# First layer's second norm reordered on VectorE: latent chunks first, then a weight piece's low part, then the context's residual; halves of the output squares added on VectorE

## The reference

```python
def _rms_norm(x, g):
    xf = x.astype(jnp.float32)
    y = xf * lax.rsqrt(jnp.mean(xf * xf, axis=-1, keepdims=True) + EPS)
    return (y * g.astype(jnp.float32)).astype(x.dtype)

def _modulate(h, shift, scale):
    return h * (1 + scale) + shift
...
        y, yc = _even_mixer(...)                      # ends in "@ w_out" for latents (y) and context (yc)
        x = x + g1 * _rms_norm(y, norm_g[1])
        h2 = _modulate(_rms_norm(x, norm_g[2]), sh2, sc2)
        x = x + g2 * _rms_norm(ffn(h2), norm_g[3])    # ffn: (silu(h @ wg) * (h @ wu)) @ wd
        if need_ctx:
            ctx = ctx + cg1 * _rms_norm(yc, norm_g[1])
            hc2 = _modulate(_rms_norm(ctx, norm_g[2]), csh2, csc2)
            ctx = ctx + cg2 * _rms_norm(ffn(hc2), norm_g[3])
```

## Time and profile before

| | |
|---|---|
| median of 3 runs | 1662.55 us (1660.24 to 1663.87) |
| profiled execution, own time | 1663.6 us |
| its span | 1661.9 us |
| TensorE busy | 1615.5 us (97%) |
| VectorE busy | 1127.4 us (68%) |
| ScalarE busy | 928.7 us (56%) |
| granted TensorE clock, mean | 0.994 of full |

### The profile page before, as it was taken

One profiled execution on the slowest core, in us unless ns is written; L12 is line 12 of the kernel. 1 busy time (PEld: TensorE's weight loads), 2 busy tenths in 40 slices (PEclk: granted clock), 3 DMA queues, 4 the chain that ended last, 5 costly groups with the idle time before them and its releaser, 6 DMA issues.

```text
span 1661.9 us, 22634 instructions
## 1 busy us (share of the span) xinstructions
PE 1615.5 (97%) x8260; PEld 1298.2 (78%) x8260; DVE 1127.4 (68%) x1503; ACT 928.7 (56%) x1335; POOL 45.1 (3%) x66
## 2 busy tenths in 40 slices
PE   7999989999999999899998999999999999999997
PEld 3884469888888888688786888888888888888886
DVE  5442433549563333553667999899999999899998
ACT  4314323622122322552566778777778777787875
POOL 0000000210000000000101000000000000000000
PEclk9999999999999999999999999999999999999999
DMA  8523631696533222352136999999999999999982
GB/s 348 206 76 127 253 128 51 220 402 239 202 140 114 102 102 101 136 210 102 29 123 271 420 421 419 392 375 382 367 389 359 399 362 399 373 377 391 374 341 78
DMA packets 68379, 427.82 MB, mean 257 GB/s; under 512 B 8785, under 2 KB 12625, under 8 KB 20305
## 3 DMA queue, kind: packets, MB, share of 16 engines
q1 hardware_dynamic: 60000, 396.93, 61.6%
q0 software_dynamic: 8304, 29.90, 4.8%
HBM read 403.20 MB, written 23.61 MB: 257 GB/s over the span
## 4 chain that ended last, share of the span: by engine, by line
PE 92%; DVE 3%; ACT 2%; DMA 1%; issue 1%; SPq 0%; DVEq 0%; ACTq 0%
PE ps L1878 27%; PE ps L1880 27%; PE ps L1879 27%; PE ps L1896 1%; PE ps L2076 1%; PE ps L1942 1%; DMA raw<-in_w 1%; PE ps L2423 1%; PE ps L2120 1%; PE ps L2141 1%; PE ps L1907 1%; PE ps L2109 1%; PE ps L2261 1%; PE ps L2145 0%; PE ps L2385 0%
## 5 line engine op out<-in xcount | busy, mean ns | idle before, releaser
L1704 DVE TENSOR_TENSOR wl<-raw,wh 128x1024 fp32r<-128x1024 f32 x522 | 615.6, 1222 | 60.2 <-ACT wh L1004 52.8
L1004 ACT ACTIVATE wh<-raw 128x1024 fp32r<-128x1024 f32 x522 | 525.0, 1057 | 95.0 <-PE ps L1880 94.9
L1878 PE MATMUL ps<-wh,ah 128*128 128x512 f32 (+1 forms) x864 | 329.5, 381 | 0.5
L1880 PE MATMUL ps<-wh,al 128*128 128x512 f32 (+1 forms) x864 | 320.5, 371 | 0.0
L1879 PE MATMUL ps<-wl,ah 128*128 128x512 f32 (+1 forms) x864 | 319.8, 370 | 0.0
L1878 PE MATMUL ps<-ah,wh 128*128 128x512 f32 (+1 forms) x784 | 282.9, 361 | 4.7 <-DVE al L1133 3.9
L1880 PE MATMUL ps<-ah,wl 128*128 128x512 f32 (+1 forms) x784 | 274.8, 350 | 0.0
L1879 PE MATMUL ps<-al,wh 128*128 128x512 f32 (+1 forms) x784 | 274.4, 350 | 0.0
L1103 DVE TENSOR_TENSOR wl<-raw,wh 128x1024 fp32r<-128x1024 f32 x120 | 141.5, 1221 | 104.4 <-ACT wh L566 104.4
L1880 PEld LDWEIGHTS ps<-wh,al 128*128 128x128 f32 x864 | 162.7, 188 | 28.8
L1878 PEld LDWEIGHTS ps<-wh,ah 128*128 128x128 f32 x864 | 162.8, 188 | 28.5 <-issue 3.6
(11 more groups left out here) (282 smaller groups left out, 1565.8 us busy)
## 6 DMA issues: line engine op xcount, KB each, us to landing
raw<-in_w SPq DMA_DIRECT2D x372, 1024.0 KB, 6.9
sent<-raw POOLq DMA_DIRECT2D x16, 512.0 KB, 24.0
back<-raw POOLq DMA_DIRECT2D x16, 512.0 KB, 25.0
x<-sent POOLq DMA_DIRECT2D x7, 512.0 KB, 11.6
back<-x POOLq DMA_DIRECT2D x7, 512.0 KB, 8.4
x<-in_x SPq DMA_DIRECT2D x2, 1024.0 KB, 8.1
raw<-in_ukv SPq DMA_DIRECT2D x1, 1024.0 KB, 7.4
ah<-flat_rows POOLq DMA_DIRECT2D x2, 512.0 KB, 7.0
```

What stands on the lines that cost most here:

```text
L1004: act.activation(wh[:, J % SPLITS, piece_half(h)], slot(J % SLOTS)[:, piece_half(h)], ACT.Copy).then_inc(w_hi, 1)
L1704: ins = dve.tensor_tensor(wl[:, J % SPLITS, piece_half(h)], slot(J % SLOTS)[:, piece_half(h)], wh[:, J % SPLITS, piece_half(h)].bitcast(F3 ...
L1878: pe.matmul(out, lh, rh, start=start, stop=False)
L1880: return pe.matmul(out, ll, rh, start=False, stop=stop)
```

## The change

VectorE gets a loop for the latents alone, which needs no root of the context. Then it splits the third gate/up piece (`split(M_GU + 2)`), and after it does the context's residual as a whole. ScalarE follows: output unit 7 and the root of `N_EYC` move into the latents' loop, the context's squares behind it. TensorE's context sums move from gate/up unit 0 into units 1 and 2, and one matmul on constants (`keep_busy`) ahead of unit 0 goes. VectorE also adds the two halves of each output unit's squares (`halves_added`), so that TensorE sums them with one matmul in place of two. `gu_half` 0 and 1 no longer stand inside the context's loop. (`cond_cleared` becomes part of `consts_set`: the same wait under another name.)

```diff
@@ T_ORDER @@
-           + [e for k in range(KD) for e in ((N_E2L, k), (N_EYC, k))] + each(N_E2C)
+           + each(N_E2L) + each(N_EYC) + each(N_E2C)
@@ ScalarE @@
             root(N_E2L)
-            out_unit(7)
-            root(N_EYC)
             for k in range(KD):
                 modulate_e2(N_E2L, k)
+                if k == 2:
+                    out_unit(7)
+                if k == 4:
+                    root(N_EYC)
+            split(M_GU + 2)
+            for k in range(KD):
                 stream_square(N_E2C, k)
-                if k == 4:
+                if k == 3:
                     rows(ATT_MODS // JOINT)
-            split(M_GU + 2)
             root(N_E2C)
             for k in range(KD):
                 modulate_e2(N_E2C, k)
-                if k in (3, 6):
-                    gu_half(k // 3 - 1)
-            for u in range(2, 6):
+            for u in range(6):
                 gu_half(u)
                 if u >= 3:
                     split(M_GU + u)
@@ VectorE @@
+            def halves_added(u):
+                p, h = OUT_UNITS[u]
+                j = SQ_AT[EY[h], p]
+                dve.wait_ge(sq_ready, j + 1)
+                dve.tensor_tensor(sq[:, j % 2, 0:TL], sq[:, j % 2, 0:TL], sq[:, j % 2, TL:T], ALU.add).then_inc(sem("halves_added"), 1)
+
+            halves_added(0)
             split(M_WOUT + 3)
+            for u in range(1, 5):
+                halves_added(u)
             dve.wait_ge(evac_act, evacs(("o", 4), "act"))
-            residual(N_EYL, lambda k: y_e[:, k, 0:TL], 0, 1)
+            residual(N_EYL, lambda k: y_e[:, k, 0:TL], 0, 1, lambda k: halves_added(5) if k == 5 else None)
+            halves_added(6)
             split(M_GU + 1)
             inverse(N_E2L)
             for k in range(KD + 1):
                 if k < KD:
                     normed_stream(N_E2L, k)
-                    if k == 0:
-                        inverse(N_EYC)
-                        dve.wait_ge(evac_act, evacs(("o", 7), "act"))
-                    if k >= 2:
-                        dve.wait_ge(res_done, RES_BEFORE[N_EYC] + k - 1)
-                    normed(N_EYC, y_e[:, k, TL:T], tmp[k % 2][:, TL:T], k)
                 if k:
                     low(N_E2L, k - 1)
-                if k < KD:
-                    residual_add(N_EYC, 0, 1, k, tmp[k % 2][:, TL:T])
+                if k == 3:
+                    halves_added(7)
+            split(M_GU + 2)
+            dve.wait_ge(mod_lo, MOD_BEFORE[N_E2L] + KD)
+            dve.wait_ge(evac_act, evacs(("o", 7), "act"))
+            residual(N_EYC, lambda k: y_e[:, k, TL:T], 0, 1)
...
-            split(M_GU + 2)
-            modulate(N_E2C, beside)
-            for u in range(2, 6):
+            modulate(N_E2C)
+            for u in range(6):
                 gu_half(u)
@@ TensorE @@
-                pe.wait_ge(sq_ready, j + 1)
-                for i in range(parts):
-                    mm = pe.matmul(ps[:, bank_of(n), 0:W], ones, sq[:, j % 2, i * W:(i + 1) * W], start=(k == 0 and i == 0),
-                                   stop=(k == count - 1 and i == parts - 1))
+                if halves:
+                    pe.wait_ge(sem("halves_added"), halves)
+                else:
+                    pe.wait_ge(sq_ready, j + 1)
+                mm = pe.matmul(ps[:, bank_of(n), 0:W], ones, sq[:, j % 2, 0:W], start=(k == 0), stop=(k == count - 1))
...
             mod_piece(ATT_MODS + 1)
-            unit_sum(7)()
-            mod_piece(ATT_MODS + 2)
...
+            first = {(1, 2): lambda: mod_piece(ATT_MODS + 2), (1, 3): unit_sum(7), (1, 5): lambda: mod_piece(ATT_MODS + 3)}
+            second = {(1, 6): lambda: context_sums(0)}
+            third = {(0, 0): lambda: context_sums(1), (0, 3): lambda: context_sums(2), (0, 6): lambda: context_sums(3),
+                     (0, 7): lambda: mod_cols(ATT_MODS // JOINT), (1, 1): lambda: context_sums(4), (1, 4): lambda: context_sums(5),
+                     (1, 7): lambda: context_sums(6, 7)}
...
-                if u == 0:
-                    keep_busy(8 % 4, 1)
                 half_piece(M_GU + m, (8 + u) % 4, h,
                            (lambda k: pe.wait_ge(mod_lo, MOD_BEFORE[(N_E2L, N_E2C)[h]] + k + 1)) if m == 0 else None,
-                           {(1, k): (lambda k=k: context_sum(k)) for k in range(1, KD)} if u == 0 else {})
-                if u == 0:
-                    sum_square(N_E2C, KD - 1)
+                           {0: first, 1: second, 2: third}.get(u, {}))
```

More of the change, by code:

```diff
@@ L615, in _ @@
             act.wait_ge(vecs_loaded, 16)
-            act.wait_ge(sem("cond_cleared"), 1)
+            act.wait_ge(consts_set, 1)
             act.activation(condP[:, 2 * (JOINT - 1):].rearrange("p (k m) -> p k m", k=KD)[:, :, 0:2], vc("cond").rearrange("p (k c) -> p k c", k=KD), ACT.Silu).then_inc(cond_ready, 1)
@@ L632, in _ @@
                 act.activation(first_sq(k), x[:, k, :], ACT.Square).then_inc(sem("first_squared"), 1)
-            act.wait_ge(consts_set, 1)
+            act.wait_ge(consts_set, 2)
             root(N_E1)
@@ L1155, in residual_add, with residual @@
                         op0=ALU.mult, op1=ALU.add).then_inc(res_done, 1)
-            def residual(n, src, layer, which):
+            def residual(n, src, layer, which, after=None):
                 inverse(n)
@@ L1167, in residual @@
                         residual_add(n, layer, which, k - 1, tmp[(k - 1) % 2])
+                    if after:
+                        after(k)
             def flat(v):
@@ L1191, in scale_post @@
                                          vc(f"norm{layer}", 16 * which, 16 * which + 16), ALU.mult)
-            dve.memset(condP, 0.0).then_inc(sem("cond_cleared"), 1)
+            dve.memset(condP, 0.0).then_inc(consts_set, 1)
             dve.memset(eps[:, :], EPS).then_inc(consts_set, 1)
@@ L1406, in gu_half @@
                                   ).then_inc(evac_dve, 1)
-            def beside(k):
-                if k in (4, 7):
-                    gu_half((k - 4) // 3)
-            split(M_GU + 2)
-            modulate(N_E2C, beside)
-            for u in range(2, 6):
+            modulate(N_E2C)
+            for u in range(6):
                 gu_half(u)
@@ L1882, in _, with sum_square @@
             summed = [0]
-            def sum_square(n, k, parts=1, first=None, last=None):
+            def sum_square(n, k, halves=None):
                 j = SQ_AT[n, k]
@@ L2152, in _ @@
             pe.wait_ge(sem("mla_pt"), len(units))
-            unit_sum = lambda u: (lambda: sum_square(EY[OUT_UNITS[u][1]], OUT_UNITS[u][0], 2))
+            unit_sum = lambda u: (lambda: sum_square(EY[OUT_UNITS[u][1]], OUT_UNITS[u][0], u + 1))
             stream_sum = lambda k: (lambda: sum_square(N_E2L, k))
@@ L2167, in _, with context_sums @@
             mod_piece(ATT_MODS + 1)
-            unit_sum(7)()
-            mod_piece(ATT_MODS + 2)
[L2171 to L2176, removed]
+            def context_sums(*chunks):
+                for k in chunks:
+                    sum_square(N_E2C, k)
+            first = {(1, 2): lambda: mod_piece(ATT_MODS + 2), (1, 3): unit_sum(7), (1, 5): lambda: mod_piece(ATT_MODS + 3)}
[3 more added lines that the diff above has]
+                     (1, 7): lambda: context_sums(6, 7)}
             def made_cols(n):
```

## The result

The changed kernel took 1669.88 us (median of 11 runs, 1666.18 to 1675.64) beside 1662.68 us (11 runs, 1660.24 to 1667.46) for the kernel before on the same chip: a ratio of 1.0038 (95% interval 1.0025 to 1.0050), which is 6.3 us slower (4.2 to 8.3). The two medians themselves differ by 7.2 us, the two means by 6.1. The forecast was 1667.8 us (+5.2) within 1664.2 to 1670.8.

The account below looks back on a forecast made before the run. TensorE, busy 97% of the span, was taken to bound. Running shifts of +1.2 (last stream sum), -4.85 (unit 1), +2.2 (ahead of unit 3) ended at +5.2 us at gate/up piece 3: 1667.8 us, range 1664.2 to 1670.8.

Parts of the forecast that it names:

- Step 1: Output projection: halves added on VectorE drop one TensorE matmul in each of seven sums, 0.43 us each, -3.0 us.
- step 2: Second output sum: unit 1's addition stands behind VectorE's split, so TensorE gets a new wait of 2.9 us.
- step 3: Sum for output unit 5: its addition stands behind chunk 4's add in the latents' residual, so +1.1 us.
- step 7: Ahead of gate/up unit 3: nothing covers the context's norm, so TensorE waits 3.2 us.
- steps 4, 5, 6, 8 and 9: Gate/up: unit 0 starts 2.4 us earlier, lasts 11.1; units 1 and 2 15.3; unit 3 7.8; table load +0.7.
- rival A: TensorE's clock falls in the new waits, the first fall costing 1.7 us: +6.9, 1669.5 us; chance 0.22.
- Rival B: The wait at unit 1's sum is absent because the split runs earlier: +2.3, 1664.9 us; chance 0.12.
- rival C: Not slower: the context's chain is hidden by an early last sum, taking off 6.0: -0.8, 1661.7 us; chance 0.08.
- rival D: Weight loads collide with GpSimd's later clearing of scratch memory, one late load costing perhaps 3 us: 1670.8; chance 0.05.
- rival E: Ahead of unit 4, the Silu idles 1.4 us more behind the table load (drain): +6.6, 1669.2 us; chance 0.03.

Follow-up runs that it names:

- e4: Kernel before, in its own order, with only the halves' additions (units 1 and 5 in time) and one matmul per sum: 1661.85 us, ratio 0.9985.
- the first: Changed kernel with VectorE's addition of unit 1's halves moved ahead of the split of the fourth projection piece: 1666.01 us, ratio 1.0005 to before.
- the second experiment: Changed kernel with unit 1's addition ahead of the split and unit 5's one chunk earlier in the latents' residual: 1665.76 us, ratio 1.0010 to before.
- the third experiment: Changed kernel with TensorE's context sums moved forward, two in gate/up unit 1, six behind unit 2's first six chunks: 1667.53 us, ratio 1.0021 to before.
- the sixth: Changed kernel with the additions for units 1 and 5 in time and the context sums early: 1662.34 us, ratio 0.9984 to before.
- e8: Changed kernel run once more, unaltered, as yardstick for the runs beside it: 1669.39 us, ratio 1.0033 to before.

## Why the prediction was right

Point by point, in the profiled execution, everything counted from the first matmul of the projection:

| step | forecast | measured |
|---|---|---|
| 1, halves | -3.0 (with unit 7's: -3.4) | -3.1 (e4) |
| 2, wait at unit 1's sum | 2.9 | 2.70 |
| 3, wait at unit 5's sum | 1.1 | 1.01 |
| 1 to 3, last stream sum | +1.2 | +1.2 (291.74 after, 292.64 in the earlier trace rows) |
| 4, gate/up unit 0 starts | -2.4 | -2.35 |
| 5, unit 0 lasts; shift at unit 1 | 11.1; -4.85 | 11.09 (to 306.53); -4.84 |
| 6, units 1 and 2 | 15.3 | 15.5 |
| 7, wait ahead of unit 3 | 3.2 | 3.10 |
| 8, unit 3 | 7.8 | 7.85 |
| 9, wait ahead of unit 4; piece 3 | 0.7; +5.2 | 0.80; +5.03 |

The mechanism and the sizes of the sum held in the stretch. Step 1 has its test in the fourth experiment, step 2 in the first, step 3 in the second, step 7 in the third, and the repairs together in the sixth; steps 4, 5, 6, 8 and 9 were read from the one profile (and came again in the others), not varied one by one. The measured time is less well met than the stretch: 1669.88 us lies within the range over the cases, but above the range of the forecast itself (1666.2 to 1669.3) and nearest to rival A's 1669.5. Taken by the ratio, +6.3, it lies inside the forecast's +3.7 to +6.7. Rival B fell with the wait of 2.70 us, rival C with the place of the last sum, rival D with the full window behind 347 us. Rival C's price was wrong too: it took 6.0 us for a context's chain that is hidden (3.2 + 2.1 + 0.7), and the third experiment, which meets its condition, gave 4.0, since the chain from the last sum to unit 4 keeps its length. For rival E the rows decide: 1.30 us from the table load's start to the Silu's, so the drain of 1.38 us that the Trainium skill names ("ScalarE: Activation LUTs", What ACT_TABLE_LOAD costs) isn't behind the load in this kernel, nor in the third experiment, where the Silu starts 1.29 us after the load's start. It isn't ahead of the load either: the copy ends at 331.52 and the load starts at 331.53.

Rival A holds in some executions. The row on which it rests was one draw: the same wait of 2.05 to 2.06 us stands in the attention part of all ten profiles, and the clock fell behind it in two (before and e8). And its price was somewhat high: such a fall takes 1.7 us of full-speed work by the windows, and 1.3 to 1.5 us of time.

The changed kernel's time grew by more than its stretch (5.0 us): by 6.1 us by the means of the first set, and by 6.5 by the medians and 6.3 by the means of the second set of 12 runs. A fall behind the 2.70 us wait, in one profile of three that have this wait unfilled, can supply some of it. But by the means such an excess over the stretch at full clock stands in kernels without that wait too: 0.6 us in the second experiment, 0.9 for the halves alone, 1.9 for the new order alone, 1.4 for both repairs. It is 2.7 in the third experiment, 0.7 with the waits filled, and absent in the first (-0.6). A mean of 12 runs is itself uncertain by some 0.6 us (a scatter of 2 us by the root of 12), that of before's 35 by 0.5. Eight of the nine differences are positive, which makes scatter alone less likely, though one set of before's runs serves four of them. They are there with and without the long waits, so the waits' falls can't be the whole of it. Where the excess comes from stays open. The end of the kernel behind piece 3 differs between single profiles by 4.5 us (1318.8 to 1323.3, with clock falls at about 815, 880 and 1650 us whose number changes), and one profile for each kernel can't average that.

## What to carry to other kernels

Work given to an idle engine costs nothing only if it is early: the addition of 0.42 us cost 3.0 because it stood in order behind a split of 2.36 that waits for something else, so look up what stands ahead of a small instruction in its engine's queue, and when that is released, before looking at its own length. The norm between these two matmul stages is a chain of fixed length (12.35 us from the last sum to the start of unit 4, in the changed kernel and with the sums early), and a reordering is worth what it does to the time of that last sum; price the chain from its start, not the gaps on the engine that waits. Taking work off the engine that bounds gave 3.1 us; the order around it, changed in the same edit, gave away more, so try the parts of such an edit apart.

## What the hardware showed unasked

Ahead of 1650 us, every fall of TensorE's granted clock in these ten profiles takes about 1.7 us of full-speed work by the windows of 10 us, or two or three times that: a stretch at 0.50 with partial slices at its ends. Where TensorE was full behind it, a fall of 1.7 us' worth cost 1.3 to 1.5 us of time; why it is less than 1.7 is not shown. The same kernel takes the falls at different places in different executions (the changed one at 218 us in one profile and not in the other), and how many it takes goes with its time: the kernel before ran in 1658 us at a mean clock of 0.998, and in 1667 to 1669 at 0.991 to 0.994. Taking (1 - clock) x span off each of its 70 runs shrinks their standard deviation from 2.85 to 1.5 us. Behind the wait of 2.05 us in the attention part it fell twice in ten profiles, after waits of 2.7 us once in three, after waits of 3.1 us in three of five. And a clock fall isn't a loss as such: where another engine sets the pace, as in unit 3, 3.4 us' worth of it vanished into the waits that were there.
